# A two-block Trainium2 kernel: the order of the expert sums of the first half, copies and diagonals on ScalarE, decays spread from two bands

## The reference, cut to what matters

```python
q = (xb @ w_query).reshape(T, PEER_HEADS, 2, PEER_HALF)            # 8 heads, 2 x 128
s = jnp.einsum('thpk,hpnk->thpn', q, sub_keys)                     # 128 keys each
top_s, top_i = lax.top_k(s, PEER_TOPK)                             # 16
...
best_s, best_pos = lax.top_k(cand_s.reshape(...), PEER_TOPK)       # 16 of 256 pairs
idx = jnp.take_along_axis(cand_i.reshape(...), best_pos, axis=-1)
gate = jax.nn.softmax(best_s, axis=-1)
u = expert_u[idx]
v = expert_v[idx]
act = jax.nn.gelu(jnp.einsum('td,thkd->thk', xb, u), approximate=False)
return jnp.einsum('thk,thkd->td', gate * act, v)
```

## Time and profile before

| what | value |
|---|---|
| runs | 3571.9, 3573.34, 3573.92 us |
| median | 3573.34 us |
| profiled execution, its own time | 3574.43 us |
| its span | 3572.7 us |
| granted PE clock, mean | 0.862 |
| PE busy | 2700.8 us (76%) |
| DVE busy | 2109.8 us (59%) |
| ACT busy | 595.0 us (17%) |
| POOL busy | 1307.6 us (37%) |
| DMA | 1006.32 MB, mean 282 GB/s |
| gathers of u, L1538 | 512, 683.7 us busy |
| gathers of v, L1538 | 512, 594.2 us busy |

### The profile page before, as it was taken

How to read it: one execution, slowest core, us unless ns; L and a number is a source line. 1 busy time by engine, 2 the same in 40 slices (tenths; PEclk the granted TensorE clock), 3 DMA queues, 4 the chain that set the end, 5 groups by cost and what they waited for, 6 DMA issues and landing times. The chain is left out here.

```text
span 3572.7 us, 44757 instructions
## 1 busy us (share of the span) xinstructions
PE 2700.8 (76%) x17746; PEld 1947.3 (55%) x17746; DVE 2109.8 (59%) x4097; ACT 595.0 (17%) x1235; POOL 1307.6 (37%) x1086
## 2 busy tenths in 40 slices
PE   6877463579960286999966576989999888787787
PEld 5766453464420174888844364778887667222232
...
GB/s 330 190 59 212 259 338 283 324 325 363 389 376 371 324 372 251 385 376 393 392 314 275 271 388 352 101 60 97 99 104 75 107 118 214 347 428 428 428 428 320
DMA packets 390751, 1006.32 MB, mean 282 GB/s; under 512 B 30381, under 2 KB 234515, under 8 KB 375699
## 3 DMA queue, kind: packets, MB, share of 16 engines
...
## 5 line engine op out<-in xcount | busy, mean ns | idle before, releaser
L1538 POOL DMA_INDIRECT ring<-in_peer_u_dram,index x512 | 683.7, 1335 | 381.2 <-DVE ring L1616 202.1
L1538 POOL DMA_INDIRECT ring<-in_peer_v_dram,index x512 | 594.2, 1161 | 293.1 <-issue 134.0
L351 PE MATMUL bank<-hT,weights 128*128 128x256 f32 x1984 | 455.1, 393 | 116.3 <-ACTq L142 55.4
L351 PEld LDWEIGHTS bank<-hT,weights 128*128 128x128 f32 x1984 | 392.1, 198 | 178.8 <-issue 108.6
L1933 PE MATMUL bank<-hT,weights 128*128 128x256 f32 x1792 | 417.9, 387 | 3.9 <-DVE weights L2131 3.9
L1933 PEld LDWEIGHTS bank<-hT,weights 128*128 128x128 f32 x1792 | 334.4, 191 | 53.3 <-DVE weights L2131 4.3
L1616 DVE SCALAR_TENSOR_TENSOR ring<-ring,h_rows_a 128x1024 f32<-128x1024 f32 x256 | 304.8, 1221 | 71.9 <-DMA ring<-in_peer_u_dram,index 69.9
L1622 DVE SCALAR_TENSOR_TENSOR h_rows_b<-ring,coef,h_rows_b 128x1024 f32<-128x1024 f32 x238 | 305.2, 1282 | 46.7 <-DMA ring<-in_peer_v_dram,index 26.6
L1616 DVE SCALAR_TENSOR_TENSOR ring<-ring,h_rows_b 128x1024 f32<-128x1024 f32 x256 | 299.9, 1223 | 7.1 <-DMA ring<-in_peer_u_dram,index 6.6
L2950 POOL IOTA mo_down<- 128x4 f32 x1 | 0.1, 145 | 792.5 <-POOLq L160 792.5
L1635 PE MATMUL bank<-ring,weights 128*128 128x512 f32 x512 | 221.9, 596 | 4.3 <-DVE weights L1610 4.3
...
## 6 DMA issues: line engine op xcount, KB each, us to landing
...
```

The source lines that it names most:

```text
L351: ins = pe.matmul(m.ps[b][:, 0:TH], m.weights[:, s, k, c * P:(c + 1) * P], rhs(k), start=(k == 0), stop=(k == k_tiles - 1))
L1538: pool.indirect_dma_start(out=self.ring[:, n % RING, :], out_offset=None, in_=self.tables[table], in_offset=bass.IndirectOffsetOnAxis(ap=s ...
```

## The change

It has four parts.

- **Order of the first half's steps.** `FRONT` is 256: all dots of both tiles come first. Then 64 groups of 2 sums of tile 0 on PE and 1 sum of tile 1 on DVE, then the last 64 sums of tile 1 on DVE. The gelu of tile 1 moves from `finish` into `key_scores`.
- **Diagonals.** ACT makes all of them (`make_diags`), after DVE has multiplied the coefficients by the gates, which a semaphore `weighed` tells. On ACT the exponential of the picker's gates stands between them; the picker's parts are split at the ninth.
- **Copies and keys.** In the second half's two projections, and in the queries, ACT copies the tiles (`copied`). The second half's keys are loaded by ACT's queue in 8 DMAs beside the output projection, over `first.h`, which is done with; the first half's by SP in 8 rather than 4.
- **SSD.** `dt`, its softplus and `acs` stand twice, on partitions 0 to 31 and 32 to 63 (16 matmuls for `dt` instead of 8, small operations on 64 partitions). The spread takes heads in turn from the two bands, each band into a bank of its own.

```diff
@@ -358,6 +359,13 @@
             else:
                 body(0, chunks, first_turn=True)
+        if copied:
+            @block.scalar
+            def _(act):
+                for t in range(n_tiles):
+                    act.wait_ge(m.tile_made, made0 + t + 1)
+                    act.copy(copied(t), m.ps[t % per_turn][:, 0:TH]).then_inc(m.tile_kept, 1)
+
         if other:
             other(block, made0, kept0)
...
@@ -366,8 +374,9 @@
             if setup:
                 setup(dve)
             for t in range(n_tiles):
-                dve.wait_ge(m.tile_made, made0 + t + 1)
-                keep(dve, t, m.ps[t % per_turn]).then_inc(m.tile_kept, 1)
+                if not copied:
+                    dve.wait_ge(m.tile_made, made0 + t + 1)
+                    keep(dve, t, m.ps[t % per_turn]).then_inc(m.tile_kept, 1)
                 if hook:
                     hook(dve, t)
                 beside(m, dve, 0.44 * k_tiles)
...
@@ -1061,21 +1070,22 @@
         project(m, w_in[0], 12, lambda k: half.h[:, k, :], KT,
                 lambda dve, t, bank: dve.tensor_copy(proj[:, t + 16, :], bank[:, 0:TH]), col0=16 * P, then=(w_in[0], 16),
-                setup=setup, hook=hook, other=other)
+                setup=setup, hook=hook, other=other,
+                copied=None if half.first else lambda t: proj[:, t + 16, :])
         project(m, w_in[0], 16, lambda k: half.h[:, k, :], KT,
                 lambda dve, t, bank: dve.tensor_copy(proj[:, t, :], bank[:, 0:TH]),
                 setup=lambda dve: short_conv(m, dve, half, cols, at, proj, carry.tail), then=(w_out[0], KT),
-                hook=hook2, other=other2)
+                hook=hook2, other=other2, copied=None if half.first else lambda t: proj[:, t, :])
         mixed = hgrn(m, half, cols, at, proj, masks, carry.hgrn, work, other3)
-        add_projected(m, half, w_out[0], mixed, KT, m.mod[:, 2 * KT:3 * KT], then)
-
-
...
+
+    def load_by(self, eng):
+        for k in range(KT):
+            eng.dma_start(self.raw[:, k, :].rearrange("p (j n) -> p j n", n=P),
+                          self.src[:, 2 * k:2 * k + 2, :]).then_inc(self.landed, 16)
     def load(self, block):
         @block.sync
         def _(sp):
-            for b in range(4):
-                sp.dma_start(self.raw[:, 4 * b:4 * b + 4, :], self.src[:, 4 * b:4 * b + 4, :]).then_inc(self.landed, 16)
+            self.load_by(sp)
+
...
         def _(pe):
-            pe.wait_ge(self.landed, 64)
+            pe.wait_ge(self.landed, 16 * KT)
             for b in range(4):
                 for j in range(4):
-                    ins = pe.transpose(m.ps[4 + b][:, j * P:(j + 1) * P], self.raw[:, 4 * b + j, :], m.ident[:, :])
+                    ins = pe.transpose(m.ps[4 + b][:, j * P:(j + 1) * P],
+                                       self.raw[:, 2 * b + j // 2, j % 2 * P:(j % 2 + 1) * P], m.ident[:, :])
                 ins.then_inc(self.turned, 1)
         @block.scalar
...
@@ -1264,13 +1282,38 @@
                 dve.tensor_copy(s_all[:, 0, n * 512:(n + 1) * 512], m.ps[n][:, :]).then_inc(first_kept, 1)
             dve.wait_ge(first_kept, 4)
             m.side.reach_front(dve)
-            for t in range(HT):
+
+        @block.scalar
+        def _(act):
+            for b in range(4):
+                act.wait_ge(made, 4 + b + 1)
+                act.copy(s_all[:, 1, b * 512:(b + 1) * 512], m.ps[4 + b][:, :]).then_inc(s_kept, 1)
+            m.side.activate(act)
+
+        for t in range(HT):
+            @block.vector
+            def _(dve):
                 if t == 1:
                     dve.wait_ge(s_kept, 4)
                 picker.load(dve, 0, s_all[:, t, :])
-                for n in range(picker.PARTS):
+                for n in range(picker.SHIFTED):
                     picker.part(dve, n, i0 + t)
                     beside(m, dve, 5.0)
+
+            @block.scalar
+            def _(act):
+                m.side.make_diags(act, m.side.n)
+                picker.exp(act, i0 + t)
+
+            @block.vector
+            def _(dve):
+                for n in range(picker.SHIFTED, picker.PARTS):
+                    picker.part(dve, n, i0 + t)
+                    beside(m, dve, 5.0)
+
+        @block.scalar
+        def _(act):
+            m.side.make_diags(act, m.side.n)
         @block.tensor
         def _(pe):
...
@@ -1473,8 +1516,8 @@
     HALF_STEPS = 2 * HT * PICKS
-    FRONT = 226
-    GROUP = 4
+    FRONT = 2 * PICKS
+    GROUP = 2
     DIAGS = 8
     SHARED = 16
...
@@ -1508,13 +1552,11 @@
         def all_of(tile, table):
             return [(tile, table, j) for j in range(PICKS)]
-        second_dots, first_sums = all_of(1, 0), all_of(0, 1)
-        steps, at = all_of(0, 0), self.FRONT - PICKS
-        steps += second_dots[0:at]
-        for j in range(0, PICKS, self.GROUP):
-            steps += first_sums[j:j + self.GROUP] + second_dots[at:at + 1]
-            at += 1
-        steps += second_dots[at:] + all_of(1, 1)
+        pe_sums, dve_sums = all_of(0, 1), all_of(1, 1)
+        steps = all_of(0, 0) + all_of(1, 0)
+        for j in range(PICKS // self.GROUP):
+            steps += pe_sums[j * self.GROUP:(j + 1) * self.GROUP] + dve_sums[j:j + 1]
+        steps += dve_sums[PICKS // self.GROUP:]
         for table in range(2):
             for tile in range(HT, TT):
                 steps += all_of(tile, table)
...
@@ -1600,15 +1642,9 @@
         coef, dots = self.coef[:, tile % HT, :], self.dots[:, tile % HT, :]
         if table == 1 and j == 0:
             dve.wait_ge(self.act_made, tile + 1)
-            c.link(dve, dve.tensor_tensor(coef, coef, self.gate[:, tile, :], ALU.mult))
-        if self.at_end(tile, table, j):
-            self.n += 1
-            return
+            dve.tensor_tensor(coef, coef, self.gate[:, tile, :], ALU.mult).then_inc(self.weighed, 1)
+            dve.wait_ge(self.weighed, tile + 1)
         if self.on_pe(tile, table, j):
-            if j >= self.DIAGS:
-                dve.wait_ge(self.summed, j - self.DIAGS + 1)
-            dve.tensor_scalar(self.diag[:, j % self.DIAGS, :], m.ident[:, :], coef[:, j:j + 1], None,
-                              ALU.mult).then_inc(self.diag_made, 1)
             self.n += 1
             return
         dve.wait_ge(self.landed[n % RING], 16 * (n // RING + 1))
...
@@ -1644,15 +1680,19 @@
         for h in range(D // 512):
             self.m.dve.mark(dve.tensor_copy(self.rows[0][:, 0, h * 512:(h + 1) * 512], self.m.ps[h][:, :]))
-    def make_diags(self, act):
-
-        for n in self.pe_steps[PICKS:]:
-            tile, table, j = self.plan[n]
-            i = self.rank[n]
-            if i >= PICKS + self.DIAGS:
+    def make_diags(self, act, end):
+
+        while self.n_diag < len(self.pe_steps) and self.pe_steps[self.n_diag] < end:
+            i = self.n_diag
+            tile, table, j = self.plan[self.pe_steps[i]]
+            diag = self.diag if i < PICKS else self.end_diag
+            if i in (0, PICKS):
+                act.wait_ge(self.weighed, tile + 1)
+            if i >= self.DIAGS:
                 act.wait_ge(self.summed, i - self.DIAGS + 1)
-            act.activation(self.end_diag[:, i % self.DIAGS, :], self.m.ident[:, :], ACT.Identity,
+            act.activation(diag[:, i % self.DIAGS, :], self.m.ident[:, :], ACT.Identity,
                            scale=self.coef[:, tile % HT, j:j + 1]).then_inc(self.diag_made, 1)
+            self.n_diag += 1
     def add_shared(self, dve):
...
@@ -1692,6 +1727,10 @@
                     if self.ending:
                         self.add_shared(dve)
+                @block.scalar
+                def _(act):
+                    self.make_diags(act, self.n)
+
                 @block.tensor
                 def _(pe):
                     self.sum_up(pe)
...
@@ -2527,14 +2570,16 @@
             def _(pe):
                 few.wait(pe)
                 for k in range(KT):
-                    ins = pe.matmul(m.ps[0][0:SH, 0:TH], w_dt[:, k, :], half.h[:, k, :], start=(k == 0), stop=(k == KT - 1))
+                    for q in range(SB):
+                        ins = pe.matmul(m.ps[0][q * SH:(q + 1) * SH, 0:TH], w_dt[:, k, :], half.h[:, k, :],
+                                        start=(k == 0), stop=(k == KT - 1))
                 ins.then_inc(made, 1)
                 up.multiply(pe, 0)
                 pe.wait_ge(soft, 9)
                 for j, src in enumerate((dt, acs)):
                     for n in range(SN):
                         ins = pe.transpose(m.ps[1][:, (j * SN + n) * SH:(j * SN + n + 1) * SH],
-                                           src[:, n * SC:(n + 1) * SC], m.ident[0:SH, 0:SH])
+                                           src[0:SH, n * SC:(n + 1) * SC], m.ident[0:SH, 0:SH])
...
@@ -2632,13 +2677,15 @@
                                 pe.wait_ge(rows_kept, 9 * n + 2 * g + 2)
                             if i >= 2:
                                 pe.wait_ge(exps, 3 * (i - 1))
```

(16 more changed lines are left out.)

78 lines of the change are left out of this document (42 added, 36 removed).

## The result

The changed kernel takes **3563.13 us** (median of 15 runs, 3558.21 to 3569.98), the kernel before 3578.88 us (15 runs beside it, 3571.0 to 3593.12). The ratio is **0.9949, 95% interval 0.9937 to 0.9961**: 18 us faster, where 57 were forecast. The profiled execution took 3558.21 us, its span is 3556.5 us, 16.2 us under that of before.

A forecast was written before the change was run, and what follows sets the result against it. PE, then DVE, summed one after the other, with DMA and POOL just under PE's pace. Terms moved the end of the first half's experts from 1225.3 to 1168.3, SSD 0: 3574.4 - 57 = 3517 us, range 3495 to 3545.

The forecast's parts named there:

- Steps 1 to 3: Before dot 226: copies to ACT in two projections (-9.5, -1.5 us), early keys and query tiles (-16.9, -2); sum -29.9 us.
- only part of the upstream gain arrives: Rival, 9%: DMA leaves little to catch up before dot 226; with half of the 30 us lost, 3532 to 3542 us.
- Step 4: First half, 30 more dots in front at the gathers' 1.29 us each: +38.7 us, to 815.2 us.
- Step 5: First half's 192 mixed steps: gathers longest at 1.308 us each, 251.1 us, plus 9 for lookups, ending at 1075.3 us.
- in step with DVE: Rival, 17%: interleaved sums hold each of the 192 mixed steps' gathers to DVE's 1.39 us, +16 us, 3533 us.
- Step 6: Last 64 sums on DVE at 1.39 us, plus 4 for w_in_2's weights: end at 1168.3 instead of 1225.3, -57 us.
- Step 7: SSD's doubled dt matmuls and spread from two bands: 0 us taken, bounds -8 and +7.
- The rival of the other side: Rival, 5%: each of 64 mixed-stretch DVE sums adds its 1.28 us to the gather beside it, +82 us, 3599 us.
- The change doesn't do what it says: Rival, 3%: no more rows side by side, PE waiting for ACT's diagonals at each exponential, some 50 us longer, 3567 us.

The follow-up runs named there:

- late: The changed kernel with the first half's 4 MB prefetch of w_in_2 held until 12 steps are left; 0.9909 of the kernel before.

## Why the prediction was wrong, step by step

- **Steps 1 to 3, upstream, -29.9 forecast, -21.1 measured.** The first projection's end moved 8.3 us (452.9 to 444.6), close to 9.5. The second gave back 2.4 where -1.5 was forecast: 95.00 us long, DMA share 0.95. From there to dot 226 the change gained 15.2 us, nearly all in the keys and queries, where 18.9 were forecast; the POOL gap of 16.90 us is gone as forecast. The rival "only part of the upstream gain arrives" was right for this part, at about two thirds, and the mechanism was right.
- **Step 4, 30 dots at 1.29.** They took 43.8 us, 1.46 each. Gathers beside dots lasted 1203 ns there. The failed term is "1.29": it was read in 784 to 806 us, 17 gathers at a mean of 17.12 / 17 = 1.01 us, the best 22 us of the front (14 gathers in the 22 us ahead of them, with weights loading).
- **Step 5, 192 steps at 1.308 and 9 us for the lookups, 260 forecast, 271.8 measured.** This is the step that failed in its reasoning: "I take 1.308, since the stretch it is from has the same mix of picks and PE rows". That stretch had 11 gathers of dots among its 51 and no sums on DVE, and its POOL instructions lasted 49.63 / 51 = 0.97 us. PE needed 237 us, close to the 221, and DVE waited, both as forecast; PE and DVE had room and the gathers had not. What the step left out is what the sums do to the gathers: of the 195 gathers begun from 829 to 1101 us, 51 were held by a sum, 15.3 us in all over their 0.94, against nothing in the sum of the prediction. The lookups held eight, as forecast, by 11.0 us where 9 were forecast; the reductions that the step counts among them hold none (the gather beside one took 0.94 us). The rival "in step with DVE" named the right price, 1.39 (269.4 us for the 192 issues, 1.40), and half of the mechanism: the held-back instruction, though the gathers were not in step with the sums, of which there was one in three steps. Its 17% was for the right price.
- **Step 6, 93 us forecast, 98.0 measured.** 64 x 1.39 assumed that DVE arrives with a backlog, as in the kernel before. It arrives waiting, and the first 36 gathers took 1.309 + 0.305 us; the rest 1.39. I had put the excess on the weights; late refutes that they alone do it.
- **Step 7, SSD, 0 forecast.** 3.2 us less in its stage, 1.1 over block 2's second half. The Trainium skill's sentence on tiles in parallel (TensorEngine Tiling (Array Packing), Key Properties) is borne out by 8.7 against 16.0 us; of the 8 us at the end that were worked out from it under half came, since DVE's products are late next.
- **The RWKV stage** was not in the prediction. Its 13.3 us are a third of the miss of 40 us in the trace, and no run here ties them to the change.
- The rival of the other side, a sum that holds a gather back by its whole length, did not come: a sum holds only a gather that begins beside it, and only for what is left of the sum, 0.14 us while DVE runs through, 0.3 in the mean where it waits for rows, and 1.0 at the longest (a gather of 1.96 us in late). "The change doesn't do what it says" did not hold either: rows of both engines stand side by side; the order is worth 5 us.

The range, 3495 to 3545, took the bounds of single terms. Of the 40.8 us missed in the span, 8.8 are upstream, 21.8 in the three terms on the gathers' pace (5.1, 11.7 and 5.0), and 10.2 behind `finish`. The three missed in one direction. Two of them, 1.29 and 1.308, were read where gathers were short (1.01 and 0.97 us) and used where they are not; the third, 1.39, was read with a backlog on DVE and used for a DVE that waits.
